# Hybrid NSA and pooling decoder block: merge-gate halves in attention's first units and not in four late ones, compression and second modulation one projection block later

## The chip, the cores and the metric

The kernel runs on one core of a Trainium2 chip. The metric is device time in microseconds (us) of one launch. Before the change it is 1578.88 us, the median of three runs (1574.45 to 1579.76). All times below are of the kernel before unless said otherwise.

## The reference, cut to what matters

One decoder layer on x of 1024 tokens by 1024 channels, all float32:

```
h = rms_norm(x, g_pre_mix) * (1 + sc1) + sh1          # shifts, scales, gates from silu(c) @ w_ada + b_ada
proj = h @ w_in                                        # q | kc | vc | ks | vs | kw | vw | nsa gates | u | merge gates
kc_c = compress(rope(kc), ...);  vc_c = compress(vc, ...)      # gelu(blocks @ w1) @ w2
o_nsa = g0 * att(q, kc_c, vc_c) + g1 * att(q, ks, vs) + g2 * att(q, kw, vw)   # compressed, selected, window of 512
o_pool = multi-scale causal mean of u (2, 4, 8, 16) minus u, then w_pool, pool_scale
merged = sigmoid(gA) * (o_nsa @ w_br_nsa) + sigmoid(gB) * (o_pool @ w_br_pool)   # gA, gB: 2048 columns of proj
x = x + gt1 * rms_norm(merged @ w_out, g_post_mix)
x = x + gt2 * rms_norm(relu((rms_norm(x, g_pre_mlp) * (1 + sc2) + sh2) @ w_fc1) ** 2 @ w_fc2, g_post_mlp)
```

The "second modulation" is the part of silu(c) @ w_ada that gives gt1, sh2, sc2 and gt2.

## The kernel before, in words

The program is one hand-written order of instructions for each engine, joined by semaphores. An engine executes its own list in order, so a wait holds up all that stands behind it. TensorE (PE) does matmuls and transposes into eight banks of PSUM (`ps`); ScalarE (ACT) and VectorE (DVE) read them; GpSimd (POOL) takes element-wise work in SBUF and some DMAs; SyncE (SP) issues the other DMAs. A float32 product is made of three matmuls on a high and a low part (`three`, L1486 to L1488): ACT copies a weight tile to its high part (`split_a`, L736), DVE or POOL subtracts to get the low part (L1074, L677), and `lo_done` tells PE that the tile is ready.

**Projection.** Twelve blocks a = 0 to 11 of 128 output columns each (`FM_COLS`: kc, vc, four of q, ks, kw, four of u) are projected channel by token: per block 48 matmuls of 512 columns. Blocks 0 and 2 to 7 get rotary embedding. For these ACT copies swapped rows (`r_swap`, L804), DVE multiplies by cos (`rope_cos_part`, L1143), POOL by sin and adds (L633, L637), ACT and DVE make high and low parts (`r_hi` L793, `r_lo` L1148), and SP stores them: q to `q_dram` (L406), keys of blocks 6 and 7 to `k_hi`, `k_lo` (L403, 16 DMAs a block). `r_hi` of a block waits until the stores of the block before it have landed, since both share two buffers (`rope_out`).

Between the blocks other work is placed by hand, with "if a == ..." in each engine's loop:

- Compression of keys and of values. SP loads shifted copies (`cmp_load`, L416, L427), DVE adds the position code (`make_blocks`, four instructions at L1160, signal `bk_made`), PE makes 16 products (`compress`, L1553) after block 4 for keys and after block 6 for values, ACT and DVE apply gelu (`gelu`, DVE L1167 to L1175, at a = 5 and 7), PE the second weights (`compress2`, after block 8).
- The second modulation. SP loads 32 pieces of w_ada, DVE adds them up (`ada2_add`, L1218, the last three at a = 6), and after block 7 PE sums over partitions in `second_modulation`: two products for the row gt1 (L1585), 16 for the columns sh2 and sc2 (L1589), then, once DVE has taken the first row (`gt_rows(0)`, L1227, signal `gt_row`), two for the row gt2.
- The pooling mixer. `pooled_part(g)` on POOL and DVE, `pooled_hi_part(g)` on ACT, and `mix(g)` on PE after blocks 9, 10 and 11, and once before attention. `mix(1)` waits for `mix_evict(0)` (ACT, L847), which waits for the last stores of key block 7, because it writes into their buffer.

SP at a = 9 waits for `gt_row` to reach 4, that is for both rows of the second modulation, stores them (L457), and only then issues `rope_stores(6)`, the 16 DMAs of block 6's keys: `k_hi` and `k_lo` lie where the sums of the second modulation were. After these stand the load of block 11's weights and `rope_stores(7)`.

**Attention.** 32 units (8 query tiles c of 128 tokens, four head pairs each). Iteration `it` of a loop over nine slots makes the scores of unit `it` (five steps: selected x2, window x2, compressed) and the transposes and value products of unit `it - 1`. For each step: scores (PE), maximum (DVE L1284), exp (ACT L899), guard (POOL L672), reciprocal and scaling (DVE L1299, L1306). For each pair of key tiles: transposes (PE L1677), `pt_hi` (ACT L918), `pt_lo` (DVE L1274), value products (PE L1693, L1694). The work grows with c, from 3 key tiles to 14.

**Merge gates.** The 2048 columns of the two merge gates are 16 more blocks of the same projection. They are made in 32 halves of 24 matmuls (`gate_part`). Halves 0 and 1 run before attention, half 31 after it, and the 29 others inside iterations of attention, eight slots with three matmuls each. `HALF_OF` says which: before, half = it - 2 for it = 4 to 32, so iterations 0 to 3 have none. In an iteration with an even half ACT splits one block of weights more (L736) and POOL makes its low part (L677). ACT evicts each half (`gate_evict`, L880) and POOL stores it (`gate_store`, L665). SP loads the weights of these blocks two halves ahead, between the loads of the queries (`load_q`).

After attention follow the merge, the output product and the MLP, which the change does not touch.

Of the kernel before, what the change touches and what calls it, by code (L numbers as in the profile page):

```python
# [21 lines left out]
P = 128  # L22
KT = D_MODEL // P
TT = SEQ // P
CH = 512
# [17 lines left out]
UNITS = TT * N_HEADS // 2  # L43
# [2 lines left out]


HALVES = 2 * N_BR
HALF_OF = dict(zip(range(UNITS + 4 - HALVES, UNITS + 1), range(2, HALVES - 1)))
assert len(HALF_OF) == HALVES - 3  # L50


# [47 lines left out]
def hybrid_block(nc, A, out):  # L100
# [25 lines left out]
    ones = place("ones", 0.5, [P, P], f32)  # L126
# [40 lines left out]
    acc2 = place("acc2", 96, [P, 4, 1024], f32)  # L167
# [161 lines left out]
    def _(sp):  # L329
# [140 lines left out]
        def load_q(c):  # L470
            if c == 0:
                for s in range(2):
                    sp.wait_ge(rope_out[s], rope_out_count(ROPES - 2 + s))
                sp.wait_ge(bkx_in, 128)
            if c >= 2:
                sp.wait_ge(score_mm, STEPS * 4 * (c - 1))
            sp.dma_start(full(q_st[:, c % 2, :, :]), q_dram[c]).then_inc(q_in[c % 2], 16)
# [6 lines left out]
        for m in range(2, N_BR):  # L484
            load_fm(N_FM + m)
            if m == 2:
                mix_store(2)
                mix_store(3)
            if m % 2 == 1 and m // 2 + 1 < TT and m >= 3:
                load_q(m // 2 + 1)  # L490

        def merge_weights(q, b):

# [88 lines left out]
    def _(pool):  # L582
# [79 lines left out]
        def gate_store(h):  # L662
            m = h // 2
            pool.wait_ge(gate_tanh, h + 1)
            pool.dma_start(g_dram[m // KT, m % KT, h % 2], g_out[:, h % 2, :]).then_inc(g_st[h % 2], 16)  # L665
# [8 lines left out]
        def split_gate_block(a):  # L674
# [2 lines left out]
            pool.tensor_tensor(a_lo[:, a % 2, :], raw[:, (R_FM + a) % 2, :], full(a_hi[:, a % 2, :]),  # L677
                               ALU.subtract).then_inc(lo_done, 1)

        for it in range(UNITS + 1):  # L680
            half = HALF_OF.get(it)
            if it < UNITS:
                guards(it, 0)
            if half is not None and half % 2 == 0 and half + 2 < HALVES:
                split_gate_block(N_FM + half // 2 + 1)
            if it < UNITS:
                for s in range(1, STEPS):
                    guards(it, s)
            if it == 0:
                gate_store(0)  # L690
                gate_store(1)
            if half is not None:
                gate_store(half)
            if it:
                v = it - 1
                pool.wait_ge(o_sum, v + 1)
                c, pair = v // 4, v % 4
                pool.dma_start(o_dram[pair * P:(pair + 1) * P, c * P:(c + 1) * P].rearrange("(h d) q -> d h q", h=2),
                               o_out[:, v % 2, :].rearrange("d (h q) -> d h q", h=2)).then_inc(o_st[v % 2], 16)
# [30 lines left out]
    def _(act):  # L730
# [119 lines left out]
        for a in range(N_FM):  # L850
            if a - 1 in FM_ROPE and 1 < a < 8:
                for ch in range(2):
                    rope_hi_part(2 * FM_ROPE[a - 1] + ch)
            for ch in range(2):
                fm_evict(a, ch)
            split_a(a + 2)
            if a == 5:
                act.wait_ge(const_in, 16 * N_SMALL)
                gelu(0)
            if a == 7:  # L860
                gelu(1)
            if a == 8:
                cmp_store()
            if a == 8:
                act.wait_ge(wp_in, 16)
                act.activation(wp_hi[:, :, :], wp_raw[:, :, :], ACT.Copy).then_inc(wp_hi_s, 1)
            if a >= 8:
                pooled_hi_part(a - 8)
            if a == 8:
                for ch in range(2):  # L870
                    rope_hi_part(ROPES - 2 + ch)
            if a >= 9:
                mix_evict(a - 9)
# [197 lines left out]
    def _(dve):  # L1071
# [165 lines left out]
        for a in range(N_FM):  # L1237
            if a - 1 in FM_ROPE and 1 < a < 8:
                for ch in range(2):
                    rope_lo_part(2 * FM_ROPE[a - 1] + ch)  # L1240
            if a in FM_ROPE:
                for ch in range(2):
                    rope_cos_part(a, ch)
            split_a(a + 2)
            if a == 7:
                gt_rows(0)
                mod2_columns()
                gt_rows(1)
            if a == 3:
                dve.wait_ge(const_in, 16 * N_SMALL)  # L1250
                make_blocks(0)
            if a == 5:
                gelu(0)
                make_blocks(1)
            for n in range(4 * KT):
                if ADD_AT[n] == a:
                    ada2_add(n)
            if a == 7:
                gelu(1)
            if a == 8:  # L1260
                cmp_store()
                dve.wait_ge(wp_hi_s, 1)
                dve.tensor_tensor(wp_lo[:, :, :], wp_raw[:, :, :], full(wp_hi[:, :, :]), ALU.subtract).then_inc(wp_lo_s, 1)
            if a >= 8:
                pooled_part(a - 8)
            if a == 8:
                for ch in range(2):
                    rope_lo_part(ROPES - 2 + ch)
# [214 lines left out]
    def _(pe):  # L1483
# [89 lines left out]
                three(ps[:, 4 + n % 2, :], wp_hi[:, g, :], wp_lo[:, g, :], pp_hi[:, sl], pp_lo[:, sl], True, True) \  # L1573
                    .then_inc(mix_mm, 1)

        def second_modulation():

            pe.wait_ge(ada2_added, 4 * KT)
            pe.wait_ge(v_lo, TT)
            pe.wait_ge(v_hi, 2 * TT)  # L1580
            for f, part in ((0, 0), (1, 3)):
                for half in range(2):
                    if f:
                        pe.wait_ge(gt_row, half + 1)
                    pe.matmul(ps[0:1, 4 + half, :], ones[:, 0:1], acc2[:, part, half * CH:(half + 1) * CH],  # L1585
                              start=True, stop=True).then_inc(gt_mm, 1)
                if f == 0:
                    for n in range(16):
                        ins = pe.matmul(ps[:, 7, n:n + 1], acc2[:, 1 + n // KT, (n % KT) * P:(n % KT + 1) * P],  # L1589
                                        ones[:, 0:1], start=True, stop=True)  # L1590
                    ins.then_inc(mod2_mm, 1)

        def gate_part(h, ks):

# [8 lines left out]
        for a in range(N_FM):  # L1603
            pe.wait_ge(lo_done, R_FM + a + 1)
            for ch in range(2):
                g = 2 * a + ch
                if g >= 4:
                    pe.wait_ge(fm_act, g - 3)
                    if a - 2 in FM_ROPE:
                        pe.wait_ge(rope_cos, 2 * FM_ROPE[a - 2] + ch + 1)  # L1610
                ins = project(a, g % 4, ch, range(KT))
                ins.then_inc(fm_mm, 1)
            if a == 4:
                compress(0)
            if a == 6:
                compress(1)
            if a == 7:
                second_modulation()
            if a == 8:
                compress2()  # L1620
            if a >= 9:
                mix(a - 9)
# [249 lines left out]
```

## Time and profile before

| | |
|---|---|
| median of three runs | 1578.88 us (1574.45, 1578.88, 1579.76) |
| span of the profiled execution | 1575.3 us (its own time is not given apart; the span stands for it) |
| PE busy | 1508.9 us, 96% |
| DVE, ACT, POOL busy | 827.5 us (53%), 565.6 us (36%), 331.8 us (21%) |
| mean granted clock of TensorE | 0.982 |
| projection blocks, first matmul of block 0 to last of `mix(3)` | about 80 to 255 us of the span |
| attention, 33 iterations | 255 to 672 us |

The span is the time from the first instruction to the last; shares are of it. A matmul's end is modelled, so that busy times of PE hold some pipeline latency. "PEclk" is the clock that TensorE was granted, as a share of 2.4 GHz; 0.50 is 1.2 GHz. Iterations of attention are told apart here by ACT's copy at their end (L947).

### The profile page before, as it was taken

The page shows a single profiled execution, that of the slowest core. Times are in us where ns is not written, and L with a number is a line of the kernel's source. Part 1 is how long each engine was busy: PE and PEld are TensorE (multiplying, and loading weights), DVE is VectorE, ACT ScalarE, POOL GpSimd, SP SyncE. Part 2 cuts the span into 40 slices and gives each one's busy share as a digit, 9 for nine tenths or more (in the row PEclk, how much of TensorE's full clock was granted, in tenths as well). Part 3 has the DMA queues.
Part 4 walks back from the last instruction along what each step waited for, and adds up shares of the span by engine and source line. Part 5 has one row for each costly group of instructions (what it writes and reads, how often), then busy time and mean ns, then how long its engine had stood idle before and what let it go on. Part 6 is the DMA issues. An engine that isn't in the chain of part 4 may idle for free.

```text
span 1575.3 us, 20573 instructions
## 1 busy us (share of the span) xinstructions
PE 1508.9 (96%) x7590; PEld 1263.8 (80%) x7590; DVE 827.5 (53%) x1445; ACT 565.6 (36%) x1092; POOL 331.8 (21%) x453
## 2 busy tenths in 40 slices
PE   2997998999999999999998999999999999999997
PEld 2886787888888888888877788888888888888886
DVE  6759736678888888854326532323232232323145
ACT  2534434555666566632226412213030302112131
POOL 3315431332322222212114201001010101011012
PEclk9999997899999999999999999999999999999999
DMA  9388772222211211265505220203030211202025
GB/s 353 76 261 250 207 187 82 59 63 66 66 40 53 58 40 38 86 189 154 180 14 187 81 66 28 81 1 106 0 91 15 68 39 40 67 17 90 0 84 183
DMA packets 129073, 148.24 MB, mean 94 GB/s; under 512 B 18405, under 2 KB 98789, under 8 KB 128999
## 3 DMA queue, kind: packets, MB, share of 16 engines
q1 hardware_dynamic: 124266, 132.64, 28.0%
q0 software_dynamic: 4736, 14.68, 2.6%
q8 instruction: 41, 0.67, 0.2%
q14 instruction: 30, 0.25, 0.1%
HBM read 115.83 MB, written 25.17 MB: 90 GB/s over the span
## 4 chain that ended last, share of the span: by engine, by line
PE 86%; DVE 6%; ACT 2%; DMA 2%; issue 2%; SPq 1%; POOL 1%; POOLq 0%; DVEq 0%; ACTq 0%
PE ps L1486 24%; PE ps L1488 24%; PE ps L1487 24%; PE ps L1677 4%; PE ps L1693 2%; PE ps L1644 2%; PE ps L1694 2%; PE ps L1645 2%; DVE acc L1218 1%; DVE ada_acc L1095 1%; DVE bk L1160 1%; PE ps L1650 1%; SPq L427 1%; DVE pt_lo L1274 1%; ACT r_swap L804 1%
## 5 line engine op out<-in xcount | busy, mean ns | idle before, releaser
L1486 PE MATMUL ps<-act_hi,a_hi 128*128 128x512 f32 x960 | 392.2, 408 | 1.6 <-DVE a_lo L1074 1.3
L1488 PE MATMUL ps<-act_hi,a_lo 128*128 128x512 f32 x960 | 375.2, 391 | 0.0
L1487 PE MATMUL ps<-act_lo,a_hi 128*128 128x512 f32 x960 | 375.0, 391 | 0.0
L1488 PEld LDWEIGHTS ps<-act_hi,a_lo 128*128 128x128 f32 x960 | 180.6, 188 | 38.5
L1486 PEld LDWEIGHTS ps<-act_hi,a_hi 128*128 128x128 f32 x960 | 181.4, 189 | 34.1 <-issue 1.9
L1053 ACT ACTIVATE relu<-ps 128x512 f32<-128x512 f32 x64 | 38.2, 597 | 468.7 <-PE ps L1488 468.7
L1487 PEld LDWEIGHTS ps<-act_lo,a_hi 128*128 128x128 f32 x960 | 181.5, 189 | 28.4
L1486 PE MATMUL ps<-b_hi,hid_hi 128*128 128x512 f32 x512 | 199.2, 389 | 0.0
L1487 PE MATMUL ps<-b_lo,hid_hi 128*128 128x512 f32 x512 | 199.2, 389 | 0.0
L1488 PE MATMUL ps<-b_hi,hid_lo 128*128 128x512 f32 x512 | 199.2, 389 | 0.0
L720 POOL TENSOR_TENSOR relu<-relu 128x512 f32<-128x512 f32 x64 | 67.3, 1051 | 583.3 <-ACT relu L1053 583.3
L1467 DVE TENSOR_TENSOR y<-ps,y 128x512 f32<-128x512 f32 x112 | 76.8, 690 | 180.9 <-PE ps L1488 180.9
L1274 DVE TENSOR_TENSOR pt_lo<-ps,pt_hi 128x512 fp32r<-128x512 f32 (+1 forms) x160 | 103.3, 645 | 20.2 <-ACT pt_hi L918 19.0
L1487 PEld LDWEIGHTS ps<-b_lo,hid_hi 128*128 128x128 f32 x512 | 96.1, 188 | 20.0
L1486 PEld LDWEIGHTS ps<-b_hi,hid_hi 128*128 128x128 f32 x512 | 96.1, 188 | 19.9
L1488 PEld LDWEIGHTS ps<-b_hi,hid_lo 128*128 128x128 f32 x512 | 96.1, 188 | 19.9
L1454 DVE TENSOR_TENSOR hid_lo<-relu,hid_hi 128x512 fp32r<-128x512 f32 x64 | 44.0, 687 | 117.8 <-ACT hid_hi L1057 117.8
L672 POOL TENSOR_SCALAR ssum<-ssum 128x1 f32<-128x1 f32 (+1 forms) x160 | 42.9, 268 | 284.8 <-ACT p_win L899 141.5
L918 ACT ACTIVATE pt_hi<-ps 128x512 fp32r<-128x512 f32 (+1 forms) x160 | 89.3, 563 | 31.3 <-PE ps L1677 30.0
L1284 DVE TENSOR_REDUCE smax<-ps 128x1 f32<-128x640 f32 (+7 forms) x128 | 89.2, 697 | 12.9 <-PE ps L1650 12.6
L1400 DVE TENSOR_TENSOR b_lo<-raw,b_hi 128x1024 fp32r<-128x1024 f32 x32 | 38.5, 1224 | 82.4 <-ACT b_hi L1031 82.4
L1644 PE MATMUL ps<-k_hi,q_st 128*128 128x320 f32 (+4 forms) x192 | 70.9, 370 | 2.2 <-ACT p_win L899 1.3
(216 smaller groups left out, 2589.9 us busy)
## 6 DMA issues: line engine op xcount, KB each, us to landing
raw<-in_w_fc SPq DMA_DIRECT2D x64, 512.0 KB, 4.0
ada<-in_w_ada SPq DMA_DIRECT2D x48, 512.0 KB, 5.8
raw<-in_w_in SPq DMA_DIRECT2D x28, 512.0 KB, 4.2
g_dram<-g_out POOLq DMA_DIRECT2D x32, 256.0 KB, 2.4
mg<-g_dram SPq DMA_DIRECT2D x16, 512.0 KB, 3.9
xt<-in_x SPq DMA_DIRECT2D x8, 512.0 KB, 7.7
q_st<-q_dram SPq DMA_DIRECT2D x8, 512.0 KB, 3.3
raw<-in_w_out SPq DMA_DIRECT2D x8, 512.0 KB, 4.4
```

The costliest lines, as they stand in the source:

```text
L672: pool.tensor_scalar(ssum[:, n % 4, 0:k], ssum[:, n % 4, 0:k], 1e-30, None, ALU.max).then_inc(guard_done, 1)
L720: pool.tensor_tensor(relu[:, n % 2, :], relu[:, n % 2, :], relu[:, n % 2, :], ALU.mult).then_inc(sq_done, 1)
L918: act.activation(pt_hi[:, n % 3, 0:w], ps[:, 4 + n % 2, 0:w], ACT.Copy).then_inc(pthi, 1)
L1274: dve.tensor_tensor(pt_lo[:, n % 3, 0:w], ps[:, 4 + n % 2, 0:w], full(pt_hi[:, n % 3, 0:w]), ALU.subtract).then_inc(ptlo, 1)
L1284: dve.tensor_reduce(smax[:, n % 4, 0:1], src, AX.XY, ALU.max).then_inc(max_done, 1)
L1454: dve.tensor_tensor(hid_lo[:, m, sl], relu[:, n % 2, :], full(hid_hi[:, m, sl]), ALU.subtract) \
L1467: dve.tensor_tensor(yt, ps[:, 4 + n % 4, :], yt, ALU.add).then_inc(y2_added, 1)
L1486: pe.matmul(dst, wh, mh, start=start, stop=False)
L1487: pe.matmul(dst, wh, ml, start=False, stop=False)
L1488: return pe.matmul(dst, wl, mh, start=False, stop=stop)
L1644: pe.matmul(dst, q, k_hi[:, 2 * branch + g, k0:k0 + wide], start=True, stop=False)
L1677: ins = pe.transpose(at, src, ident[:, :])
```

## The change

`HALF_OF` now gives halves to iterations 0 to 24, 26, 28, 30 and 32 (half = it + 2 up to 24, then 27, 28, 29, 30). Iterations 25, 27, 29 and 31 have none. The number of halves is the same. POOL stores halves 0 and 1 before its loop, and SP loads the queries one pair of weight blocks later in its list.

In the projection PE makes the first compression product after block 5 instead of 4, the second after block 7 instead of 6, the first part of the second modulation (row gt1 and columns) after block 7 as before but behind the second compression, and its second part (row gt2) after block 8. ACT and DVE follow: `gelu(0)` and `make_blocks(1)` stand at a = 6 instead of 5, and `gt_rows(1)` at a = 8.

```
--- before.py
+++ after.py
@@ -46,7 +46,8 @@
 
 
 HALVES = 2 * N_BR
-HALF_OF = dict(zip(range(UNITS + 4 - HALVES, UNITS + 1), range(2, HALVES - 1)))
+UNFILLED = (25, 27, 29, 31)
+HALF_OF = dict(zip([it for it in range(UNITS + 1) if it not in UNFILLED], range(2, HALVES - 1)))
 assert len(HALF_OF) == HALVES - 3
 
 
@@ -486,8 +487,8 @@
             if m == 2:
                 mix_store(2)
                 mix_store(3)
-            if m % 2 == 1 and m // 2 + 1 < TT and m >= 3:
-                load_q(m // 2 + 1)
+            if m % 2 == 1 and m >= 5:
+                load_q(m // 2)
 
         def merge_weights(q, b):
 
@@ -677,6 +678,8 @@
             pool.tensor_tensor(a_lo[:, a % 2, :], raw[:, (R_FM + a) % 2, :], full(a_hi[:, a % 2, :]),
                                ALU.subtract).then_inc(lo_done, 1)
 
+        gate_store(0)
+        gate_store(1)
         for it in range(UNITS + 1):
             half = HALF_OF.get(it)
             if it < UNITS:
@@ -686,9 +689,6 @@
             if it < UNITS:
                 for s in range(1, STEPS):
                     guards(it, s)
-            if it == 0:
-                gate_store(0)
-                gate_store(1)
             if half is not None:
                 gate_store(half)
             if it:
@@ -854,7 +854,7 @@
             for ch in range(2):
                 fm_evict(a, ch)
             split_a(a + 2)
-            if a == 5:
+            if a == 6:
                 act.wait_ge(const_in, 16 * N_SMALL)
                 gelu(0)
             if a == 7:
@@ -1242,22 +1242,21 @@
                 for ch in range(2):
                     rope_cos_part(a, ch)
             split_a(a + 2)
-            if a == 7:
-                gt_rows(0)
-                mod2_columns()
-                gt_rows(1)
             if a == 3:
                 dve.wait_ge(const_in, 16 * N_SMALL)
                 make_blocks(0)
-            if a == 5:
+            if a == 6:
                 gelu(0)
                 make_blocks(1)
             for n in range(4 * KT):
                 if ADD_AT[n] == a:
                     ada2_add(n)
             if a == 7:
+                gt_rows(0)
+                mod2_columns()
                 gelu(1)
             if a == 8:
+                gt_rows(1)
                 cmp_store()
                 dve.wait_ge(wp_hi_s, 1)
                 dve.tensor_tensor(wp_lo[:, :, :], wp_raw[:, :, :], full(wp_hi[:, :, :]), ALU.subtract).then_inc(wp_lo_s, 1)
@@ -1573,22 +1572,22 @@
                 three(ps[:, 4 + n % 2, :], wp_hi[:, g, :], wp_lo[:, g, :], pp_hi[:, sl], pp_lo[:, sl], True, True) \
                     .then_inc(mix_mm, 1)
 
-        def second_modulation():
-
-            pe.wait_ge(ada2_added, 4 * KT)
-            pe.wait_ge(v_lo, TT)
-            pe.wait_ge(v_hi, 2 * TT)
-            for f, part in ((0, 0), (1, 3)):
-                for half in range(2):
-                    if f:
-                        pe.wait_ge(gt_row, half + 1)
-                    pe.matmul(ps[0:1, 4 + half, :], ones[:, 0:1], acc2[:, part, half * CH:(half + 1) * CH],
-                              start=True, stop=True).then_inc(gt_mm, 1)
-                if f == 0:
-                    for n in range(16):
-                        ins = pe.matmul(ps[:, 7, n:n + 1], acc2[:, 1 + n // KT, (n % KT) * P:(n % KT + 1) * P],
-                                        ones[:, 0:1], start=True, stop=True)
-                    ins.then_inc(mod2_mm, 1)
+        def second_modulation(f):
+
+            if f == 0:
+                pe.wait_ge(ada2_added, 4 * KT)
+                pe.wait_ge(v_lo, TT)
+                pe.wait_ge(v_hi, 2 * TT)
+            for half in range(2):
+                if f:
+                    pe.wait_ge(gt_row, half + 1)
+                pe.matmul(ps[0:1, 4 + half, :], ones[:, 0:1], acc2[:, 3 * f, half * CH:(half + 1) * CH],
+                          start=True, stop=True).then_inc(gt_mm, 1)
+            if f == 0:
+                for n in range(16):
+                    ins = pe.matmul(ps[:, 7, n:n + 1], acc2[:, 1 + n // KT, (n % KT) * P:(n % KT + 1) * P],
+                                    ones[:, 0:1], start=True, stop=True)
+                ins.then_inc(mod2_mm, 1)
 
         def gate_part(h, ks):
 
@@ -1610,12 +1609,13 @@
                         pe.wait_ge(rope_cos, 2 * FM_ROPE[a - 2] + ch + 1)
                 ins = project(a, g % 4, ch, range(KT))
                 ins.then_inc(fm_mm, 1)
-            if a == 4:
+            if a == 5:
                 compress(0)
-            if a == 6:
+            if a == 7:
                 compress(1)
-            if a == 7:
-                second_modulation()
+                second_modulation(0)
+            if a == 8:
+                second_modulation(1)
             if a == 8:
                 compress2()
             if a >= 9:
```

The places in the order of instructions on which the prediction rests are these.

DVE in the projection, from the rotary part and weight split (L1143, L1074) of block 5 on; `gelu_t` is gelu(0), `acc` the sums of the second modulation, `ada<-ps,ada` the two rows gt:

```order
 L1143 TENSOR_TENSOR r_cos<-ps,cos 128x512 x2
 L1074 TENSOR_TENSOR a_lo<-raw,a_hi 128x1024
+L1218 SCALAR_TENSOR_TENSOR acc<-ada,col,acc 128x1024 x3
+L1148 TENSOR_TENSOR r_lo<-r_cos,r_hi 128x512 x2
+L1143 TENSOR_TENSOR r_cos<-ps,cos 128x512 x2
+L1074 TENSOR_TENSOR a_lo<-raw,a_hi 128x1024
 L1167 TENSOR_TENSOR gelu_t<-gelu_x 64x126
 L1169 TENSOR_SCALAR gelu_t<-gelu_t 64x126
```

The first gelu, and with it `make_blocks(1)` right behind, has moved past three additions and past all of block 6's work on DVE.

PE at the end of block 7 (the rows `act_hi,a_hi` are the first of a block), before:

```order
L1488 MATMUL ps<-act_hi,a_lo 128x512
L1585 MATMUL ps<-acc,ones 1x512 [waits v_hi,v_lo,ada2_added]
L1585 MATMUL ps<-acc,ones 1x512
L1589 MATMUL ps<-ones,acc 128x1 x16
L1585 MATMUL ps<-acc,ones 1x512 [waits gt_row] x2
L1486 MATMUL ps<-act_hi,a_hi 128x512 [waits rope_cos,fm_act,lo_done]
```

and now (line numbers are one lower), at the end of block 7 and, below the dots, of block 8:

```order
L1487 MATMUL ps<-act_hi,a_lo 128x512
L1552 MATMUL ps<-bk,cw 64x126 [waits gelu_c,bk_made,cw_in]
L1552 MATMUL ps<-bk,cw 64x126 x15
L1584 MATMUL ps<-acc,ones 1x512 [waits v_hi,v_lo,ada2_added]
L1584 MATMUL ps<-acc,ones 1x512
L1588 MATMUL ps<-ones,acc 128x1 x16
L1485 MATMUL ps<-act_hi,a_hi 128x512 [waits rope_cos,fm_act,lo_done]
...
L1584 MATMUL ps<-acc,ones 1x512 [waits gt_row] x2
L1558 MATMUL ps<-gelu_t,w2k 64x126 [waits gelu_d]
```

Block 8 now stands behind `bk_made` of the values, and the row gt2 behind block 8.

ACT in a late iteration that loses its half (the widths 56 and 896 are those of c = 6):

```order
 L918 ACTIVATE pt_hi<-ps 128x256
 L899 ACTIVATE p_win<-ps,negm 128x640
-L880 ACTIVATE g_out<-ps 128x512
 L904 ACTIVATE p_cmp<-ps,negm 128x56 x2
 L947 ACTIVATE o_tmp<-ps 64x256
```

The eviction has gone from there, as have 24 matmuls on PE; nothing of the iteration's own work has moved.

## Rows read from the trace of the kernel before

**Rows 1.** The page, busy time, share and instructions of each engine.

```profile
PE 1508.9 (96%) x7590; PEld 1263.8 (80%) x7590; DVE 827.5 (53%) x1445; ACT 565.6 (36%) x1092; POOL 331.8 (21%) x453
```

**Rows 2.** Windows: stretches of the projection, then of attention's first iterations; columns in row one.

```profile
core 0: us, PE busy (x) PEld busy (x) DVE busy (x) ACT busy (x) POOL busy (x), PEclk, DMA share, GB/s
134.60:141.37 6.77, 0.00 (x0) 0.03 (x1) 6.77 (x6) 2.46 (x5) 3.93 (x2) 0.88 0.88 214
141.37:147.46 6.09, 6.09 (x33) 5.92 (x33) 6.09 (x6) 4.56 (x7) 2.13 (x1) 0.57 0.60 186
170.13:173.70 3.57, 3.57 (x32) 3.40 (x32) 3.57 (x4) 1.90 (x4) 0.00 (x0) 1.00 1.11 329
185.20:190.74 5.54, 5.54 (x36) 3.90 (x36) 5.22 (x6) 3.89 (x7) 3.96 (x3) 1.00 0.38 96
191.17:194.54 3.37, 3.37 (x5) 0.34 (x5) 1.37 (x4) 0.00 (x0) 1.87 (x5) 0.53 0.00 0
206.22:255.09 48.87, 48.87 (x218) 40.46 (x216) 25.19 (x30) 18.77 (x30) 13.55 (x7) 1.00 0.53 148
255.09:260.53 5.44, 3.71 (x24) 3.04 (x23) 3.69 (x18) 3.41 (x14) 0.85 (x4) 0.88 0.68 193
260.53:285.10 24.57, 20.28 (x91) 17.77 (x91) 16.64 (x71) 10.78 (x46) 5.80 (x19) 0.50 0.10 29
```

**Rows 3.** Timeline of DVE in the projection: start us, us, what, idle before.

```profile
135.54 5.68 DVE L1160 TENSOR_TENSOR bk<-bkx,pe_col 128x504 f32<-128x504 f32 x4
...
148.14 2.00 DVE L1074 TENSOR_TENSOR a_lo<-raw,a_hi 128x1024 fp32r<-128x1024 f32 x1
...
162.22 1.33 DVE L1074 TENSOR_TENSOR a_lo<-raw,a_hi 128x1024 fp32r<-128x1024 f32 x1 [0.40 <-ACT a_hi L736]
163.48 1.37 DVE L1167 TENSOR_TENSOR gelu_t<-gelu_x 64x126 f32<-64x126 f32 x1
...
166.26 3.77 DVE L1160 TENSOR_TENSOR bk<-bkx,pe_col 128x504 f32<-128x504 f32 x4
...
178.99 1.53 DVE L1074 TENSOR_TENSOR a_lo<-raw,a_hi 128x1024 fp32r<-128x1024 f32 x1 [0.40 <-ACT a_hi L736]
```

**Rows 4.** Timeline of ACT in the projection, at blocks 6 and 9.

```profile
172.40 0.63 ACT L793 ACTIVATE r_hi<-r_cos 128x512 fp32r<-128x512 f32 x1 [1.01 <-DMA q_dram<-r_lo]
173.05 4.82 ACT L804 ACTIVATE r_swap<-ps 32x512 f32<-32x512 f32 x8
...
217.44 0.60 ACT L815 ACTIVATE pu<-ps 128x512 f32<-128x512 f32 x1 [2.22 <-PE ps L1488]
```

**Rows 5.** Timeline of SP's DMA queue at the stores of block 6's keys.

```profile
195.35 0.23 SPq L457 DMA_DIRECT2D gt_dram<-ada  x1
196.70 2.42 SPq L403 DMA_DIRECT2D k_hi<-r_hi  x4
```

**Rows 6.** DMA issues by line: count, KB each, median us to landing.

```profile
k_lo<-r_lo SPq DMA_DIRECT2D x16, 128.0 KB, 2.3
```

**Rows 7.** Timeline of DVE after block 8: split of block 10, pooled low part of group 1.

```profile
207.33 2.14 DVE L1074 TENSOR_TENSOR a_lo<-raw,a_hi 128x1024 fp32r<-128x1024 f32 x1 [10.32 <-ACT a_hi L736]
...
225.37 1.23 DVE L1208 TENSOR_TENSOR pp_lo<-ps_a,pp_hi 128x1024 fp32r<-128x1024 f32 x1 [1.13 <-ACT pp_hi L837]
```

**Rows 8.** Windows: iterations 4, 25, 27, 29 and 31 of attention, columns as in Rows 2.

```profile
285.10:296.94 11.84, 11.84 (x60) 10.09 (x60) 6.99 (x24) 5.68 (x17) 4.04 (x7) 0.80 0.31 92
...
550.39:565.69 15.30, 15.30 (x105) 13.21 (x104) 12.81 (x29) 9.18 (x22) 2.69 (x7) 1.00 0.07 22
...
581.05:596.42 15.37, 15.37 (x105) 13.29 (x104) 12.80 (x29) 9.22 (x22) 2.69 (x7) 1.00 0.07 23
...
612.05:627.91 15.86, 15.86 (x108) 13.70 (x106) 13.46 (x29) 9.62 (x21) 3.05 (x7) 1.00 0.07 22
...
643.99:660.07 16.08, 16.08 (x111) 14.14 (x111) 13.53 (x29) 9.72 (x21) 3.04 (x7) 1.00 0.09 25
```

**Rows 9.** Waits in 260.53 to 285.10 us: in total, times, longest.

```profile
PEld ps L1693 <- DVE pt_lo L1274: 4.8, 6, 1.0
```

## Prediction

> **What bounds the kernel now.** I read the page first: PE is busy 96% of the span and no other engine above 53% [rows 1]. So a change of order can gain only where PE waits or runs at 1.2 GHz, and can lose wherever it makes PE wait. The windows show where that is. In the projection PE stands still for 6.77 us before the first compression, while DVE makes its blocks; the product then takes 6.09 us at a clock of 0.57, where the second takes 3.57 us at 1.00; and the last two sums of the second modulation take 3.37 us at 0.53 [rows 2]. From 206.22 to 255.09 us PE has no idle time at all. In attention iteration 0 and iterations 1 to 3, which have no gate half, take 5.44 and 24.57 us, the latter at a clock of 0.50 throughout. Late in attention PE is busy all of 15.3 to 16.1 us an iteration, and DVE 12.8 to 13.5 us of it [rows 8]. The change touches these three places.
>
> **The change, part A: the projection up to block 9.** The 48.87 us hold four and a half times 48 matmuls (blocks 9 to 11, gate halves 0 and 1, the mixes); a block is 10.9 us, a half 5.45 us, a `mix` 1.4 us. Now the order of PE, step by step.
> - Block 4 ends at 134.60 us. Block 5 needs its low part on DVE, which stands directly before the blocks for the keys, so it starts at 135.6 us [rows 3] and ends at 146.5. The compression is ready since 141.2 and takes 3.6 us at full clock: 150.1. Block 6 needs the low part that ends at 150.1 [rows 3] and ends at 161.0.
> - Block 7 needs the low part that began at 162.22 before. It may come up to 0.8 us earlier; I take block 7 as 162.7 to 173.6 us. Before, it ended about 184.6 us. Up to here 11 us are gained.
> - Then PE meets the second compression. Its blocks now stand on DVE behind block 6's work, and that is not paced by PE: ACT's `r_hi` of block 5 starts at 172.40 when stores of q land, the swap of block 6 runs 173.05 to 177.9 [rows 4], and DVE's split of block 8 ends at 180.5 [rows 3]. None of these was waiting for PE, so PE being early moves none. Gelu follows (163.48 to 166.26, 2.8 us) and the blocks (3.77 us): 187.0 us. PE waits 13.4 us.
> - The compression after such a wait I price like the first one now, 6.1 us [rows 2]; at full clock it would be 3.6. So 193.1 us. The three additions end before that. Row gt1 and the columns take 5.54 us [rows 2]: 198.6 us. Block 8 takes 10.9, and I add 1.0 because the clock fell right after these sparse sums before (0.53 in the next row): 210.5 us. The row gt2 at full clock is 3.37 times 0.53, 1.8 us; `compress2` some 0.8 us. Block 9 starts at 213.1 us instead of 206.2.
> A costs **6.9 us**. Its bounds: 3.5 (full clock in both places) and 10 (the blocks at the pace of the first set, 5.68 us, instead of 3.77). In that set POOL was busy 3.93 of 6.77 us beside DVE, in the 3.77 one it was idle as far as its window shows [rows 2]. The Trainium skill (GPSIMD Engine Reference, section Specifications) says that GpSimd and VectorE share the SBUF interface when a DVE instruction has two SBUF inputs, as these have; by that rule the blocks would cost 5.7 us if POOL worked beside them, and A 8.8. POOL's work for block 6 ends before they start, so I keep 3.77.
>
> **Part B: what is queued behind the row gt2.** SP stores both rows and only then issues the 16 key stores of block 6: before at 195.35 and 196.70 us [rows 5], with PE at block 8. Now the row comes after block 8, whose end I call T (210.5 us). DVE first splits block 10: 207.33 with block 8 ending about 205.5, so T + 1.8 to T + 3.9 [rows 7], then the row, 1.3 us: T + 5.2. The stores start T + 6.5, take 16 times 0.62 us, and land 2.3 us later [rows 5, 6]: T + 18.9. ACT's `r_hi` of block 7 waits for this landing, and ACT evicts block 9 only after it, by T + 20.7. From the start of that second eviction to the pooled low part it takes 217.44 to 226.6, 9.2 us [rows 4, 7]: T + 29.3. `mix(1)`'s second half also waits until block 7's key stores have landed, T + 30.3. PE would reach it, unhindered, at T + 1.8 + 0.8 + 10.9 + 1.4 + 10.9 + 0.7 = T + 26.5. B costs **3.7 us**, between 0 (shorter stores) and 7 (the clock falls in the wait).
> Later loads still fit: block 12's weights are loaded at about T + 28, needed at T + 43.
>
> **Part C: the early iterations.** They get four halves, 21.8 us of matmuls. At 1.2 GHz PE was busy 20.28 us in iterations 1 to 3 [rows 2], 10.1 at full clock, 3.4 each; with a half 8.9 us each. DVE's 16.64 us for the three fit in 26.7. Iteration 0: its scores are at most 3.71 us of busy time, overlapped; about 7.4 us. Iteration 4 took 11.84 us at 0.80 [rows 8], 9.4 at full clock. Together 43.5 against 41.85 us: C costs **1.7 us**, bounds 0.5 and 4. The stores of halves 0 and 1 go before the loop on POOL: both halves are out before its first guard, so nothing.
>
> **Part D: the late iterations.** Iterations 25, 27, 29, 31 take 62.6 us and lose 5.45 us of matmuls each. PE alone would need 9.9 to 10.6 us; DVE's 12.81, 12.80, 13.46 and 13.53 us (52.6 in all) now bind. DVE cannot be gapless: at an iteration's end it waits for ACT's copy, and on the way for PE and ACT. I allow 1.0 us each of the 2.5 us idle now: 56.6 us. D gains **6.0 us**, bounds 3 and 9. The query loads still come an iteration or more ahead.
>
> **Sum.** 6.9 + 3.7 + 1.7 - 6.0 = **+6.3 us**: 1575.3 becomes 1581.6 us of span. The median of the runs is 3.6 us above that span; put on it, 1578.9 + 6.3 = 1585.2 us. A measurement of this kernel tells about 0.3% from no change, 4.7 us: below 1574.2 is faster, above 1583.6 slower.
>
> The clock decides D. In iterations 1 to 3 it stayed at 0.50 for 24.57 us although no wait of PE was longer than 1.0 us [rows 9]; the work at full clock would fill 41% of that time. In the late iterations it would fill some 70%, and no row shows such a stretch. The Trainium skill (TensorE: Matmul & The Clock Gate, section Why this matters for your kernels) advises only against idle gaps over about 3 us. By that rule the late iterations keep 2.4 GHz and D stands; by it the early ones should have kept it too, and the trace disagrees, so a rival below gets a chance.
>
> **Rivals.**
> 1. *Faster: DVE and ACT come early with PE.* If the stores of q land sooner, since the queues differ, DVE's split of block 8 could end near 170 us and the second compression would not wait. PE would then lose only the 6.8 us wait and 2.5 us of low clock it has now, less 1.3 before block 5: A is -8; B stays, since it hangs on the end of block 8 alone. Sum -8 + 3.7 + 1.7 - 6 = -8.6: 1570 us. It decides if the second `bk` is made before 176 us. Against it: the waits named at 172.40 are on DMA, not PE. Chance 0.12.
> 2. *No change: the stages cancel.* The mechanism is as forecast, but A is near 4.5, B near 1 (ACT gets its buffers in time), C near 1, and DVE runs with almost no gaps, D -7.5: -1, 1578 us. It decides if the late iterations end below 13.6 us on the mean and B's wait is hidden by block 10. For it: the bounds of A and D. Chance 0.28.
> 3. *Slower still: the clock falls late.* With the gate halves gone, iterations 25, 27, 29 and 31 drop to 1.2 GHz, where PE needs up to 20 us each. It would rise again in the filled ones between. If half of each ran so, PE would need 15 us plus about 2 us in the next: instead of -1.5 each, +1.5. Sum 6.9 + 3.7 + 1.7 + 6 = +18: 1597 us. Chance 0.08.
> 4. *The change does not do what it says:* the early halves wait for weights, as the split of block 14 must come in iteration 0. Its load waits only for the split of block 12, about T + 33, 244 us; the iteration starts near 266. No chance of its own.
>
> **How the numbers follow.** The forecast has 0.52; its own range from the bounds is 1580 to 1591. I predict 1585 us. The range of 8 in 10 reaches down over the second rival, 1571, and up to 1593; left out are most of rivals 1 and 3. Faster: rival 1 and a quarter of rival 2, 0.19. Same: most of rival 2 and the low end of the forecast, 0.29. Slower: the rest of the forecast and rival 3, 0.52.
>
> **What would show it.** In the profile after: PE idle of about 13 us before the second compression and about 1 before block 5; the first one at full clock in 3.6 us; the key stores of block 6 starting about 20 us later; a wait of 3 to 4 us before `mix(1)`; iterations 1 to 3 at clock 1.00 and just below 9 us; iterations 25 to 31 (odd) at 13.8 to 14.5 us with DVE busy over 90% and clock 1.00. A second wait under 5 us, or a low clock late in attention, would make the prediction wrong.

## The result, and the profile after

The changed kernel takes 1590.37 us, the median of four runs (1589.84 to 1591.65), against 1577.88 (1574.45 to 1579.76, four runs) before: ratio 1.0082, 95% interval 1.0067 to 1.0096. It is slower, by 12.5 us; 6.3 were forecast. The profiled run took 1590.68 us. Its span is 1588.9 us, 13.6 above that of before; the table below adds up in spans, the forecast and the experiments are held against medians. Its page begins:

```profile
span 1588.9 us, 20573 instructions
PE 1502.1 (95%) x7590; PEld 1253.3 (79%) x7590; DVE 832.8 (52%) x1445; ACT 564.7 (36%) x1092; POOL 328.4 (21%) x453
```

PE is busy 6.8 us less than before [rows 1], with a higher mean clock (0.988 against 0.982), and yet the span is longer: the loss is waiting. The windows show where (columns as in rows 2): four of the projection, then iteration 0, iterations 1 to 3, iteration 4, and iterations 25, 27, 29 and 31.

```profile
145.90:149.60 3.70, 3.70 (x34) 3.43 (x32) 3.70 (x6) 0.00 (x0) 2.34 (x2) 1.00 0.96 278
173.10:186.86 13.76, 0.02 (x2) 0.03 (x1) 9.46 (x14) 10.45 (x19) 6.64 (x5) 0.59 0.62 188
186.86:193.24 6.38, 6.38 (x33) 6.21 (x33) 6.38 (x7) 2.60 (x4) 0.98 (x1) 0.55 0.01 3
198.80:211.32 12.52, 12.52 (x48) 9.92 (x48) 1.43 (x7) 0.91 (x2) 0.00 (x0) 0.86 0.00 1
267.79:276.40 8.61, 8.33 (x49) 6.82 (x48) 5.80 (x19) 4.86 (x16) 3.53 (x6) 1.00 0.81 244
276.40:304.58 28.18, 27.33 (x164) 22.85 (x164) 18.14 (x71) 13.70 (x50) 8.59 (x21) 1.00 0.17 54
304.58:314.36 9.78, 9.67 (x58) 8.03 (x58) 8.13 (x24) 5.67 (x17) 4.65 (x8) 1.00 0.45 139
567.83:581.88 14.05, 11.05 (x81) 9.10 (x80) 12.62 (x29) 8.36 (x21) 2.69 (x7) 1.00 0.07 23
597.23:611.27 14.04, 11.27 (x81) 9.20 (x80) 12.62 (x29) 8.36 (x21) 2.65 (x7) 1.00 0.08 26
626.91:641.73 14.82, 11.94 (x88) 9.83 (x87) 13.25 (x29) 8.89 (x21) 2.88 (x7) 1.00 0.07 22
657.54:672.35 14.81, 12.17 (x90) 10.22 (x90) 13.23 (x29) 8.89 (x20) 2.84 (x7) 1.00 0.13 42
```

PE stands for 13.76 us before the second compression, runs it at a clock of 0.55, and has 0.86 in block 8. The early iterations are longer than before and at full clock; the four late ones shorter, with DVE busy 90% of them. The timeline of PE shows the sums and the wait behind them (start us, us, what, idle before and its releaser):

```profile
186.86 6.45 PE L1552 MATMUL ps<-bk,cw 128*64 128x126 f32 x32 [13.74 <-DVE bk L1160]
193.24 1.88 PE L1584 MATMUL ps<-acc,ones 128*1 128x512 f32 x4
195.05 3.73 PE L1588 MATMUL ps<-ones,acc 128*128 128x1 f32 x32
...
239.94 0.50 PE L1485 MATMUL ps<-pp_hi,wp_hi 128*128 128x512 f32 x1 [2.80 <-DVE pp_lo L1208]
```

What made the second `bk` late stands in ACT's timeline, then in DVE's:

```profile
172.36 0.63 ACT L793 ACTIVATE r_hi<-r_cos 128x512 fp32r<-128x512 f32 x1 [0.77 <-DMA q_dram<-r_lo]
173.01 4.79 ACT L804 ACTIVATE r_swap<-ps 32x512 f32<-32x512 f32 x8
177.83 1.06 ACT L736 ACTIVATE a_hi<-raw 128x1024 fp32r<-128x1024 f32 x1
...
224.51 0.63 ACT L793 ACTIVATE r_hi<-r_cos 128x512 fp32r<-128x512 f32 x1 [4.38 <-DMA k_lo<-r_lo]
229.64 0.63 ACT L793 ACTIVATE r_hi<-r_cos 128x512 fp32r<-128x512 f32 x1 [4.49 <-DMA k_lo<-r_lo]
```

```profile
178.92 1.47 DVE L1074 TENSOR_TENSOR a_lo<-raw,a_hi 128x1024 fp32r<-128x1024 f32 x1 [0.39 <-ACT a_hi L736]
180.31 1.34 DVE L1167 TENSOR_TENSOR gelu_t<-gelu_x 64x126 f32<-64x126 f32 x1
...
183.05 3.70 DVE L1160 TENSOR_TENSOR bk<-bkx,pe_col 128x504 f32<-128x504 f32 x4
```

`r_hi` and the swap start within 0.04 us of where they did before [rows 4], though PE had come 11 us early: the landing of q's stores sets them. In SP's list the last q stores before that `r_hi` stand behind the loads of the shifted copies and of w_ada, and their issue begins at 162.36 us before and 162.40 us now. Then the queue of SP, whose `k_hi` began at 196.70 before [rows 5]:

```profile
216.37 0.23 SPq L458 DMA_DIRECT2D gt_dram<-ada  x1
217.72 2.41 SPq L404 DMA_DIRECT2D k_hi<-r_hi  x4
...
236.32 2.52 SPq L404 DMA_DIRECT2D k_lo<-r_lo  x4
```

The stores of block 6's keys start 21.0 us later. Those of block 7 start 13.4 us later (228.52 us against 215.15) and are issued until 238.8; ACT waits on their landings (the two `r_hi` above, 8.9 us), and `mix(1)` behind ACT.

| part | forecast | measured in the spans | from |
|---|---|---|---|
| A, block 9's start | +6.9 | +7.5 | 213.76 against 206.22 |
| B, from there to attention | +3.7 | +5.0 | 54.03 against 49.10 |
| C, iterations 0 to 4 | +1.7 | +5.0 | 46.6 against 41.6 |
| D, iterations 25, 27, 29, 31 | -6.0 | -4.9 | 57.7 against 62.6 |
| tail after attention | 0 | +1.3 | 904.9 against 903.5 |

Attention is taken here to start with its first matmul, at 255.32 us before and 267.79 us now. The five sum to +13.9; iteration 30 is 0.3 us shorter. The tail hardly is the change's work: in both kernels the clock falls once near 850 us, beside a wait of PE of 4.5 to 4.6 us, for 3.4 us before and 6.8 us after, and other runs below show either length (3.4 us in experiment 6, 6.8 in the rest). What sets the length is not shown.

### The profile page after: what moved, and what is told of

Its sections match the earlier page's. It is cut to its first block, busy times and chain, and to the rows that moved or that the text cites. A ratio compares the mean times of both kernels' runs of the same rounds, so it can differ in the third digit from the quotient of the medians.

```text
span 1588.9 us, 20573 instructions
## 1 busy us (share of the span) xinstructions
PE 1502.1 (95%) x7590; PEld 1253.3 (79%) x7590; DVE 832.8 (52%) x1445; ACT 564.7 (36%) x1092; POOL 328.4 (21%) x453
## 4 chain that ended last, share of the span: by engine, by line
PE 80%; DVE 9%; SPq 3%; ACT 3%; issue 2%; DMA 2%; POOL 0%; POOLq 0%; ACTq 0%; DVEq 0%
PE ps L1485 23%; PE ps L1487 22%; PE ps L1486 22%; PE ps L1677 3%; PE ps L1644 2%; PE ps L1693 2%; PE ps L1694 2%; PE ps L1645 1%; DVE smax L1283 1%; DVE ada_acc L1095 1%; SPq L404 1%; DVE acc L1218 1%; DVE pt_lo L1273 1%; SPq L428 1%; DVE p_sel L1305 1%
## 5 line engine op out<-in xcount | busy, mean ns | idle before, releaser
L1693 PE MATMUL ps<-pt_hi,v_st 128*128 128x256 f32 x264 | 71.1, 291 | 2.1 <-DVE pt_lo L1273 1.9
```

Source lines behind the costliest of these rows:

```text
L1693: pe.matmul(dst, v, pt_hi[:, n % 3, 256 * x:256 * x + 256], start=first, stop=False)
```

## The experiments

Each was timed beside the kernel before; the granted clock and every length of an iteration are from the one profiled execution of each. Iterations are told apart as before by ACT's copy (L947).

**1 and 2. Each half of the change alone.** First attention's part alone, the projection as before; then the projection's part alone. The edits are the matching hunks of the diff above, undone; below, where the steps of the projection stand in 1, and the placing of the halves in 2 (with it SP's loads of the queries and POOL's stores of halves 0 and 1 go back too):

```
# 1, as before                            # 2, against the changed kernel
 a == 5: gelu(0)   a == 4: compress(0)    -UNFILLED = (25, 27, 29, 31)
 a == 6: compress(1)                      +HALF_OF = dict(zip(range(UNITS + 4 - HALVES, UNITS + 1), range(2, HALVES - 1)))
 a == 7: second_modulation()
```

> The kernel before with the new placing of the merge-gate halves alone; the projection is that of before. Theory: the two parts add up. In the profile after, iterations 0 to 4 took 46.7 us instead of 41.85 (+4.8) and iterations 25, 27, 29, 31 took 57.7 instead of 62.6 (-4.9), so this part by itself should be worth 0 within 1.5 us. Rival: the early iterations were slow because the projection ended late (queues and stores still busy); then this kernel should have iterations 1 to 3 near 8.9 us and be 2 us or more faster than before.

> The kernel before with the new order of the projection alone; the halves of the merge gates stand as before. Theory: the whole loss sits here, +12.5 us, from 6.9 to 7.5 us before block 9 and about 5 us between block 9 and attention. Rival: the loss comes from both parts meeting; then it is under 9 us here.

Measured: attention alone 1577.74 us, ratio 1.0001 (0.9993 to 1.0010); the projection alone 1590.30 us, 1.0078 (1.0064 to 1.0091). So the whole loss is the projection's, and C and D cancel. In the first the iterations have the lengths of the changed kernel (9.4 us for 1 to 3, 14.05, 14.05, 14.82, 14.82), so they are not long because the projection ended late. Its profiled run, 1582.38 us, is the slowest of its eleven (the others 1576.99 to 1579.76): there attention starts at 260.11 us, 4.8 later than before, with a wait of PE of 2.6 us for the last additions of the second modulation; that is a difference between runs, since the projection is that of before. In the second attention starts at 267.32 us, 12.0 us late, and its unfilled iterations are at half clock again, as before [rows 2]:

```profile
272.76:297.00 24.24, 19.70 (x91) 17.29 (x90) 16.23 (x70) 11.09 (x45) 5.85 (x20) 0.52 0.11 31
```

**3. Part B undone:** the row gt2 back at a = 7, on PE and on DVE, with the rest of the change kept.

```
-            if a == 8:
                 second_modulation(1)        # PE; DVE's gt_rows(1) likewise from a == 8 to 7
```

> The changed kernel with one thing undone: PE makes the row gt2 directly behind the columns, before block 8, and DVE takes it at a = 7. Theory (part B of the prediction): the key stores of block 6 start about 13 us earlier, the wait before mix(1) of 2.8 us and the low clock after it go, and the kernel is 4 to 5 us faster than the changed one, although block 8 now starts 3.5 us later. Rival: the stores are not what mix(1) waits for; then the wait stays and the kernel is the same or up to 2 us slower than the changed one.

Measured: 1585.24 us, ratio 1.0044 (1.0031 to 1.0057), 5.1 us below the changed kernel. `k_hi` starts at 203.44 instead of 217.72, PE no longer waits at `mix(1)`, attention starts at 262.97 instead of 267.79. Block 9 starts at 213.88 us, within 0.12 us of the changed kernel, and from there to attention it is 49.09 us, as before the change (49.10). SP's queue:

```profile
202.08 0.23 SPq L458 DMA_DIRECT2D gt_dram<-ada  x1
203.44 2.41 SPq L404 DMA_DIRECT2D k_hi<-r_hi  x4
```

The key stores behind `gt_row` are the cause of B, and B is worth about 5 us, not 3.7 (4.9 in the spans, 5.1 by the medians, 4.7 when each median is set against the kernel before of its own rounds).

**4. Part A's cause undone:** `gelu(0)` and `make_blocks(1)` back at a = 5, in front of block 6's work on ACT and DVE.

```
-            if a == 6:
+            if a == 5:
                 gelu(0)
                 make_blocks(1)
```

> The changed kernel with one thing undone: ACT and DVE make gelu(0) and the blocks of the values at a = 5 again, while PE's order stays the new one. Theory (part A): the second set of blocks is ready near 169 us, PE goes from block 7 into the second compression without a wait at 173 us, and waits instead some 8 us for the last additions of the second modulation (185 us); block 8 starts near 193 us instead of 198.8, and the kernel is 5 to 7 us faster than the changed one. Rival: the wait of 13.7 us is only moved, since DVE's list is as long as before; then it is within 2 us of the changed one.

Measured: 1587.91 us, ratio 1.0062 (1.0049 to 1.0075), only 2.5 us below the changed kernel (2.0 when each is set against the kernel before of its own rounds), where 5 to 7 were expected. PE's timeline tells why:

```profile
174.82 3.67 PE L1552 MATMUL ps<-bk,cw 128*64 128x126 f32 x32
186.14 3.57 PE L1584 MATMUL ps<-acc,ones 128*1 128x512 f32 x4 [7.65 <-DVE acc L1218]
189.64 6.99 PE L1588 MATMUL ps<-ones,acc 128*128 128x1 f32 x32
```

The second compression waits for nothing and runs at full clock, 12 us earlier. But PE then meets the sums of the second modulation, whose last additions (L1218) stand on DVE behind block 6's rotary work: a new wait of 7.65 us, after which the sums run at a clock of 0.50 throughout, 10.5 us where the changed kernel needs 5.5:

```profile
186.14:196.60 10.46, 10.46 (x37) 7.30 (x37) 6.27 (x7) 3.81 (x7) 6.36 (x7) 0.50 0.19 52
```

So the wait named `bk` was right as a cause, and wrong as a price: it covered a second one. Block 9 starts at 212.09 us, 1.7 earlier than in the changed kernel, and from there to attention it is 53.99 us, as there (54.03): B does not depend on this wait.

**5. Both waits avoided:** as in 4, and the first part of the modulation on PE and DVE behind block 8, before the row gt2; attention as before.

```
-                second_modulation(0)        # a == 7
             if a == 8:
+                second_modulation(0)
                 second_modulation(1)
```

> Attention as before. In the projection the first compression goes after block 5, the second after block 7, but gelu(0) and the blocks of the values stay at a = 5 on ACT and DVE, and all sums of the second modulation go after block 8. Theory: what the changed order lost was PE standing in front of DVE's list; here PE should wait 0 before both compressions, about 4 us before block 8 (its weights split at 180.5 us), start block 9 near 200 us instead of 206.2, and lose about 3 us again at mix(1), since the key stores start near 202 us: 3 to 4 us faster than before. Rival: the sparse sums or the later stores cost as much as the waits that go; then it is within 1 us of before, or slower.

Measured: 1576.56 us against 1577.52 (33 runs), ratio 0.9990 (0.9981 to 0.9999): the loss is gone, and 1.0 us is gained, where 3 to 4 were expected. Block 9 starts at 204.52 us, 1.7 before that of the kernel before and not near 200: the sums, now in front of it, take 9.0 us, and from block 9 to attention it is 50.53 us, 1.4 longer than before. What is left of the waits moved to block 8, whose weights' low part stands on DVE behind the same stores of q:

```profile
174.87 3.67 PE L1552 MATMUL ps<-bk,cw 128*64 128x126 f32 x32
182.23 0.50 PE L1485 MATMUL ps<-act_hi,a_hi 128*128 128x512 f32 x1 [3.68 <-DVE a_lo L1074]
...
200.43 3.57 PE L1584 MATMUL ps<-acc,ones 128*1 128x512 f32 x4
```

The row gt2 runs at half clock (3.57 us against 1.88) right behind the columns, as it did before. Attention starts at 255.05 us, 0.3 before that of the kernel before.

**6, 7 and 8. Where the unfilled iterations lie.** Attention as in the change, the projection as before, with four other iterations unfilled; in 7 and 8 SP's loads of the queries are placed anew, so that they come in time.

```
-UNFILLED = (25, 27, 29, 31)
+UNFILLED = (1, 3, 29, 31)      # 6;  7: (5, 7, 9, 11);  8: (13, 15, 17, 19)
```

> Projection as before; iterations 1, 3, 29 and 31 of attention have no gate half, 0 and 2 have one. It asks what a half in every second early iteration does to the clock. Theory: matmuls of a half in between hold 2.4 GHz, iterations 1 and 3 then take 6.5 to 7.5 us instead of 9.4 filled, and the kernel is 3 to 5 us faster than before. Rival: the clock falls in iterations 1 and 3 all the same, as it did in the four unfilled ones of the kernel before; then they take about 8 us, the filled one between them over 10, and the kernel is within 1.5 us of before.

> Projection as before; iterations 5, 7, 9 and 11 have no gate half, all others to 32 but none after have one; SP's loads of the queries are placed to come in time. Here PE's own work fills a smaller share of an unfilled iteration (4.2 us of a possible 7.5 in iteration 5) than late in attention. Theory: DVE and latency set 7.5 to 8 us in iterations 5 and 7 and about 9.5 in 9 and 11, instead of 9.65 and 11.3, the clock stays up, and with +4.8 us early the kernel is 2 to 3 us faster than before. Rival: the clock falls in them; then the kernel is slower than before by 2 us or more.

> Projection as before; iterations 13, 15, 17 and 19 have no gate half. Theory: DVE sets them, its 10 us of iterations 13 and 15 and 11.3 us of 17 and 19 plus about 1.3 us of waits: 11.3 and 12.6 us instead of 12.7 and 14.2, a gain of 6 us against 4.8 us lost early, 1 us faster than before. Rival: the waits grow as PE's share falls and the gain stays under 4 us: same as before or slower.

Measured: 1580.31 us, 1.0018 (1.0009 to 1.0027); 1581.33 us, 1.0020 (1.0010 to 1.0031); 1579.49 us, 1.0009 (0.9999 to 1.0019); before, 1577.52. They were expected 3 to 5, 2 to 3 and 1 us faster than before and are 2.8, 3.8 and 2.0 us slower; none is better than 25, 27, 29 and 31. In all three the clock falls inside or behind an unfilled iteration: at 271.4 and 285.0 us in 6, at 347.1 in 7, at 422.7 and 443.2 in 8. The windows show it in 7, in the unfilled iteration 9 (339.33 to 350.14 us), before and after the clock falls:

```profile
339.33:347.10 7.77, 4.54 (x30) 3.31 (x29) 6.07 (x18) 4.24 (x11) 2.07 (x6) 1.00 0.13 43
347.10:353.90 6.80, 6.46 (x25) 5.56 (x26) 4.85 (x17) 3.55 (x11) 1.27 (x4) 0.50 0.05 12
```

and in 8, at the end of the unfilled iteration 15:

```profile
422.70:426.10 3.40, 3.09 (x12) 2.69 (x13) 2.45 (x8) 1.92 (x9) 1.07 (x3) 0.50 0.76 248
```

At full clock an iteration left unfilled saves 2.1 us in 7 (iteration 7, 7.57 us against 9.63), and the filled one behind it gives 0.4 of that back (10.57 against 10.14, also at full clock); where the clock falls, iteration 9 takes 10.81 against 11.19, and the filled one behind it 13.51 against 11.48. In 6 the filled iteration between the two unfilled ones takes 10.82 us, against 9.42 in the changed kernel. Taken together, iterations 5 to 12 gain 2.8 us in 7 and iterations 13 to 20 gain 4.4 in 8, less than the 5 us that the filled early ones cost. This is rival 3's mechanism, in another place.

**9 and 10. A version that might beat both:** the unfilled iterations 0, 27, 29 and 31, since an unfilled iteration 0 takes some 3 us less and an unfilled 25 only 1.2; in 9 with the projection of 5, in 10 with that of before.

```
-UNFILLED = (25, 27, 29, 31)
+UNFILLED = (0, 27, 29, 31)
```

> The projection as in the run with the first part of the second modulation after block 8 (that part of the order alone was 1.0 us under before, ratio 0.9990), and attention as in the change but with the unfilled iterations 0, 27, 29 and 31 instead of 25, 27, 29 and 31. Theory 'each iteration costs the larger of PE's and DVE's work' gives: iteration 0 stays at 5.4 us (5.44 before, 8.7 in the change), 1 to 3 take 9.4 each (28.2 against 24.6), iteration 4 takes 9.8 (11.84 before), iterations 27, 29 and 31 lose 1.2 each (14.05, 14.8, 14.8): +3.6 - 2.0 - 3.6 = -2.0 us, with the -1.0 of the projection 3.0 under before, 1574.5 us, ratio 0.9981. Theory 'the clock takes it back': the unfilled iteration 0 leaves PE at half clock into iteration 1, as at 271.4 us with 1 and 3 unfilled (3.4 us of low clock, some 1.7 lost), and the ratio is 0.999 or above.

> The projection as before, attention with the unfilled iterations 0, 27, 29 and 31. Theory 'larger of PE's and DVE's work': 2.0 us under before, about 1575.5, ratio 0.9987 (the same edit with 25 in place of 0 gave 1.0001; iteration 0 gives back 3.3 us, iteration 25 takes 1.2 more). Theory 'the clock takes it back': 1577 or more, ratio within 0.0005 of 1.

Measured: 1578.17 us, ratio 0.9998 (0.9987 to 1.0008), and 1577.71 us, 1.0003 (0.9994 to 1.0012), beside 1577.88: no gain. In 10 the clock falls where iteration 1 begins, which makes iterations 0 and 1 together 16.1 us; in 9 it doesn't, and they take 14.6:

```profile
255.98:260.90 4.92, 3.10 (x24) 2.44 (x22) 3.51 (x18) 2.98 (x13) 1.15 (x5) 1.00 0.96 305
260.90:264.30 3.40, 3.35 (x11) 2.59 (x10) 1.78 (x7) 2.17 (x7) 0.84 (x3) 0.50 0.07 21
```

So in 10 low clock takes 1.5 of the 2 us that were to be gained. In 9 the clock falls late instead, in the unfilled iteration 29, behind waits of PE of at most 1.1 us:

```profile
616.20:619.60 3.40, 3.40 (x18) 3.00 (x17) 3.09 (x7) 1.69 (x3) 0.26 (x1) 0.51 0.00 0
```

There it costs nothing: the iteration takes 14.82 us, as at full clock in the changed kernel, since DVE binds it. For 9 the profiled run took 1574.45 us, as forecast, but its eleven runs fall into two groups: five from 1573.78 to 1576.13 with a mean clock of 0.989 to 0.990, six from 1578.17 to 1579.34 with 0.986 to 0.989. The slower six have on the whole more low clock (one of them, at 0.989, does not stand out); in which place stays open, as only one run, of the quicker five, has a trace. So experiment 9 gives no gain that can be counted on, and it isn't shown why its median lies 3.7 us above the forecast.

## Why the prediction was right or wrong

The side was right and so were the mechanisms; the time, 1585, was 5 us low (inside the range). The median rose by 12.5 us where the sum said 6.3. Every term missed to the same side, so no error hid another: in the spans C by 3.3 us, B by 1.3, D by 1.1, A by 0.6, and 1.3 in the tail, where nothing was expected.

- **A, right: +7.5 against +6.9.** Block 5 waits 1.10 us for its low part; the first compression takes 3.70 us at full clock; the second waits 13.74 us until 186.86 (187.0 was forecast), since "none of these was waiting for PE" held to 0.04 us; it then takes 6.4 us at 0.55. The blocks took 3.70 us, the pace of the second set, as assumed. POOL was busy only 0.66 us beside them, so the rule of the Trainium skill (GPSIMD Engine Reference, section Specifications), that GpSimd and VectorE share the SBUF interface when a DVE instruction has two SBUF inputs, wasn't put to the test. Two details of the step are not sound: the window of rows 2 that was to show POOL idle beside the blocks before, 170.13 to 173.70, begins where they end (POOL's timeline does show it idle from 164.7 to 175.5), and the upper bound of 10 us should be the 8.8 that its own reason gives. The 0.6 us missing are mostly low clock in block 8: 12.5 us, where 11.9 was taken. Experiment 4 adds what the step didn't see: the additions are as late as the blocks.
- **B, the mechanism right, the size low: +5.0 against +3.7.** (16 stores of 0.62 us and 2.3 us to land make T + 18.7, not 18.9, which changes nothing.) The forecast had the start of `k_hi` at T + 6.5; it was 217.72 with T at 211.3, T + 6.4. The wait itself is shorter than forecast (2.80 us). What was missed is the low clock that follows it, from 240.4 for 3.4 us (1.7 lost), named only as the upper bound. Experiment 3 gives about 5 us for the whole part.
- **C, the term that was mis-sized: +5.0 against +1.7.** The step "20.28 us ..., 10.1 at full clock, 3.4 each" halves a busy time at 1.2 GHz. Iterations 1 to 3 took 9.4 us each, not 8.9, and iteration 0 took 8.6, not 7.4. PE was busy 27.33 of their 28.18 us: take off three halves of 5.45 and 11.0 are left, not 10.1, and 0.85 of idle time was not allowed for at all. An iteration's small matmuls don't all halve when the clock doubles. The groups of the same instructions in iterations 1 to 3 show it, first before at 0.50, then now at 1.00 (number, busy us and mean ns of one):

```profile
L1650 PE MATMUL ps<-mask_diag,ident_b 128*128 128x128 bf16 x12 | 4.0, 330 | 0.0
L1658 PE MATMUL ps<-mask_cmp,ident_b 128*128 128x8 bf16 x6 | 1.1, 189 | 0.0
...
L1650 PE MATMUL ps<-mask_diag,ident_b 128*128 128x128 bf16 x12 | 2.8, 230 | 0.0
L1658 PE MATMUL ps<-mask_cmp,ident_b 128*128 128x8 bf16 x6 | 1.1, 179 | 0.0
```

In iteration 0 the step took the scores as mostly hidden: 7.4 us less a half of 5.45 leaves 2.0 for them, and PE was busy 8.33 us, 2.9 beside the half.
- **D, right within its bounds: -4.9 against -6.0.** DVE binds, as said: 12.62, 12.62, 13.25, 13.23 us busy, 90%. It is idle 1.4 to 1.6 us an iteration instead of the 1.0 allowed, and PE now waits for its `pt_lo` before the transposes:

```profile
PEld ps L1677 <- DVE pt_lo L1273: 3.0, 3, 1.3
```

That is iteration 25: in total, times, longest; some of it is hidden behind matmuls still running. The clock stayed at 1.00 in the late iterations of this kernel and of experiment 1. The Trainium skill (TensorE: Matmul & The Clock Gate, section Why this matters for your kernels) advises against idle gaps over about 3 us. The late iterations of this kernel agree with it; experiments 8 and 9 don't: in 8 the clock fell at the end of iteration 15, in which no wait of PE was longer than 1.5 us, and in 9 in iteration 29, with none over 1.1 us. Here the measurement decides.
- **Rival 1** failed on the point named for it: `bk` was made at 186.8, not before 176. **Rival 2** described attention alone (C and D cancel, ratio 1.0001) but not the projection. **Rival 3** didn't occur in 25 to 31 of this kernel; that it can is shown by experiment 9, where it cost nothing. **Rival 4:** no wait of PE for weights in iterations 0 to 4; the longest of PE from 267.79 to 314.36 us is 0.3 us, for DVE's scaling.

## What to carry to other kernels

When a step is moved down an engine's list, look up what paces the list at its new place: here PE came 11 us early and the step's inputs did not, since they stood behind work paced by the landing of stores, and the wait that is named hides the next one (removing the first of 13.7 us returned 2.5). A row that another queue's stores wait for is part of that queue's schedule: one late sum of 1.9 us moved 16 stores by 21.0 us and 16 more by 13.4. Filling idle slots early in exchange for slots late pays only the difference of what the two kinds cost, here nothing. And a busy time measured at half clock must not be halved to get that at full clock.

## What the runs showed of the hardware that was not expected

- The 16 products of one column each with their loads (L1589 before, L1588 in the variants) take 3.73 us at full clock in the changed kernel and 6.99 us at 0.50 in experiment 4, and the clock stayed low for 20.5 us from 180.5 there, through the 10.46 us of sums in which PE was busy all the time.
- The clock fell, for 3.4 or 6.8 us, in stretches where PE waited at most 1.5 us at a time (experiments 7 and 8), and in experiment 9 in iteration 29 with waits of at most 1.1 us, but not in iterations 25 to 31 of the changed kernel with waits of up to 1.3 us. The length of a single wait does not tell the two apart.
- Runs of the same kernel can differ: the two groups of experiment 9 are 3.8 us apart in their means.
- A low clock cost nothing where DVE was the limit and much where PE was: 3.4 us of it in the unfilled iteration 29 of experiment 9 left that at 14.82 us, while the filled iteration 10 of experiment 7, with 3.8 us of it, took 13.51 us against 11.48.
